# Two chained blocks in float32 on one core: order of work at retention's entry, in attention's last step, and around the norm factors

## The chip, the core and the metric

The program runs on 1 core of a Trainium2 chip. The metric is the device time of one execution in microseconds. The median of three runs is 2414.36 us (2413.3 to 2414.92). The kernel uses five instruction streams: TensorE (PE), VectorE (DVE), ScalarE (ACT), GpSimd (POOL) and SyncE (SP, which only issues transfers). They share SBUF and PSUM and order themselves by semaphores.

## What is computed

The input is x (1024 tokens, width 1024), with two blocks of layers behind each other. Cut to what matters:

```python
def first_block(x, ...):
    p = rms_norm(x, norm_mix_pre) @ w_in
    p_rw, p_ret, g_rw, g_ret = split(p)
    y_rw  = rwkv7_mixer(p_rw, ...)          # 8 heads of 64, chunked recurrence, head norm, gate
    y_ret = retention_mixer(p_ret, pos)     # 8 heads, rotary, decay mask, group norm, silu gate
    merged = sigmoid(g_rw) * (y_rw @ w_branch_rw) + sigmoid(g_ret) * (y_ret @ w_branch_ret)
    h = x + rms_norm(merged @ w_out, norm_mix_post)
    f = (gelu(gate) * val) @ w_down         # gate, val: 3-tap causal convolution of rms_norm(h) @ w_up
    return h + rms_norm(f, norm_ffn_post)

def second_block(x, ...):
    pool_u, pool_gate, q, k, v, attn_gate = split(rmsnorm(x, norm_pre) @ w_in_2)
    pool_out = pool_mixer(pool_u) * silu(pool_gate)
    attn_out = swa_sink_attention(q, k, v, sinks) * silu(attn_gate)   # window 128, 8 heads, 2 kv heads
    y = concat([pool_out, attn_out]) @ w_out_2
    return x + rmsnorm(y, norm_post)
```

## The kernel before

**Layout and products.** Features lie on the 128 partitions, the 1024 tokens along the free axis. Every large product is made from split operands: a float32 number is kept as a high part (`whi`, `xhi`, type fp32r) and a low part (`wlo`, `xlo`), and three matmuls of 128x128 by 512 columns are added in PSUM: high by high, high by low, low by high. A tile of 128 output features over a contraction of 1024 is thus 24 matmuls for each half of 512 tokens.

**Weights.** SP streams blocks of 128x1024 into `wraw` (two slots). POOL splits each: a cast (L402) into `whi` and a subtraction (L404) into `wlo`, then raises `w_ready`. It may overwrite a slot only after PE has raised `w_used` at a matmul of the following block: that is, while PE works from one slot, the other is split. `w_used` is attached to the first matmul of a block, but in the last product of the second block (`last_block`) blocks 0 and 1 are interleaved, and there it comes at the matmul k = 3 of block 0 and k = 4 (`LATE`) of block 1.

**The rwkv stage.** A loop over 4 pairs of heads. In each, PE makes 6 products for the mixer and then 10 later ones (`later_products`) whose matmuls are dealt out one by one as fillings (`fill(n)`) between the small matmuls of the recurrence. Their results go through `psg[0]`/`psg[1]`, are scaled by DVE into `stage` (`normed_half`, L1443) and stored by ACT (`store_later`). At the pair's end come: the sums of squares (L544), DVE's and ACT's head factor, its spread over partitions by 8 transposes (L551), then on DVE the multiply of YB by it (L1558), on ACT scale and bias (L2308), on DVE the addition of the bonus and the gate (L1560, L1562), the store of YB to `yrw_scratch`, and `normed_half` and the store of product 9. YB is a tile of its own name for EN; its last content, of pair 3, stays in SBUF as `yrw[3]`.

**Retention.** `ret_values(p, h)` (L853) brings the values of head h to token order, into `psb`, but for the first pair's head 1 into `psg[1]`, after product 9 has left it. ACT copies them (`values`, L2320), PE turns the keys (`ret_keys`, L860), ACT copies these, PE makes the scores (L886) into `psa` and `psg[1]` and the chunk states (L893), DVE masks the scores (RP, L1609) and runs the states (RS, L1615), PE makes the outputs (L903, L908). Between them stand the matmuls of y_rw @ w_branch_rw as fillings (`fill_branch`, L816). Their operand `xhi` is cast by ACT (L2341), `xlo` subtracted by DVE (`operand_low`, L1595), four each.

**Norm factors.** A factor per token is summed with small matmuls, its root is taken on ACT and DVE, and it is spread to all partitions by transposes (`half_spread`, `spread_of`). These stand between the half blocks of the first products after each norm (`up_block`, `mix_block`, 24 matmuls each, k = 0 to 7).

**Out blocks.** `out_block(n)` is a half tile of merged @ w_out, block 0 waiting before each k for `op_split`, the low half of that feature of `merged` (`merged_low`, L1655).

**Attention.** 16 steps. In each PE makes the scores of the next step, runs 10 fillings, waits for the probabilities (`ap_ready`, DVE L2112), turns them (L1282), runs 6 fillings and multiplies by the values (L1290). The last step, which has no scores to make, runs 24 fillings:

```python
                    else:
                        fill(24 if n == 4 * PAIRS - 1 else 10)
                    pe.wait_ge(sem("ap_ready"), n + 1)
```

The fillings come from one chain of the remaining projections and the first 8 blocks of the last product, in this order: block 0 without k = 7, block 1 with k = 0 to 3, block 0's k = 7, the rest of block 1, blocks 2 to 7.

## Time and profile before

| | us |
|---|---|
| median of 3 runs | 2414.36 |
| lowest, highest | 2413.3, 2414.92 |
| the profiled execution's own time | 2412.11 |
| its span | 2410.3 |
| PE busy | 2356.0 (98%) |
| DVE busy | 1377.7 (57%) |
| POOL busy | 790.9 (33%) |
| ACT busy | 658.0 (27%) |

The profile is of one execution. The times in its rows count from the start of the span; the execution's own time is 1.8 us more than the span. The busy time of PE is counted from modelled ends, so a busy PE may still be one that runs at its lower clock: the windows give the clock that was granted, as a share of 2.4 GHz. In a timeline, a bracket at a row's end gives how long the engine had been idle, and who released it; the same engine's next row shows when it went on.

### The profile page before, as it was taken

What the parts mean: (1) busy time and instruction counts of PE and PEld (TensorE: products, weight loads), DVE (VectorE), ACT (ScalarE), POOL (GpSimd) and SP (SyncE); (2) the same over time, 40 slices, a digit from 0 to 9 for tenths busy, and PEclk for the clock granted to TensorE, in tenths of its full rate; (3) what the DMA queues carried; (4) which work ended last, traced back from release to release, by engine and by line L of the source; (5) the groups of instructions that cost most, each with busy time, mean ns of one, the idle gap of its engine ahead of it and who ended that gap; (6) DMA issues with size and microseconds to landing.
All of it is one profiled execution on the core that took longest, in us unless ns stands there. A gap on an engine that the chain in (4) does not pass through costs nothing.

```text
span 2410.3 us, 33719 instructions
## 1 busy us (share of the span) xinstructions
PE 2356.0 (98%) x12944; PEld 1918.1 (80%) x12944; DVE 1377.7 (57%) x1562; ACT 658.0 (27%) x1064; POOL 790.9 (33%) x420
## 2 busy tenths in 40 slices
PE   7999999999999999999999999999999999999997
PEld 6888888888887887887787788888878787777775
DVE  7755465446545644766558744544541387657766
ACT  4312121121113112443242211111122445114441
POOL 2311231222113114113465333333334445422154
PEclk9999999999999999999999999999999999999998
DMA  3211211121111115645434111111124333211023
GB/s 143 68 53 53 71 55 51 53 71 53 56 59 62 62 45 180 210 145 202 155 130 150 53 47 49 44 52 44 46 76 141 120 120 95 64 63 44 27 79 113
DMA packets 61904, 205.22 MB, mean 85 GB/s; under 512 B 6240, under 2 KB 10464, under 8 KB 61152
## 3 DMA queue, kind: packets, MB, share of 16 engines
q1 hardware_dynamic: 40560, 138.76, 18.5%
q10 hardware_dynamic: 21232, 64.80, 7.3%
q8 instruction: 91, 1.49, 0.3%
q14 instruction: 21, 0.17, 0.0%
HBM read 167.36 MB, written 36.18 MB: 84 GB/s over the span
## 4 chain that ended last, share of the span: by engine, by line
PE 90%; DVE 6%; ACT 2%; DVEq 1%; issue 1%; DMA 0%; POOL 0%; ACTq 0%; POOLq 0%
PE psg L477 10%; PE psg L482 10%; PE psg L481 10%; PE psg L609 7%; PE psg L614 6%; PE psg L616 6%; PE psa L709 1%; PE psg L1205 1%; PE psg L1198 1%; PE psg L571 1%; PE psg L574 1%; PE psg L1203 1%; PE psg L575 1%; PE psb L696 1%; PE psg L1249 1%; PE psg L1243 1%
## 5 line engine op out<-in xcount | busy, mean ns | idle before, releaser
L402 POOL CAST whi<-wraw 128x1024 fp32r<-128x1024 f32 (+1 forms) x176 | 192.2, 1092 | 1397.2 <-PE psg L609 516.8
L404 POOL TENSOR_TENSOR wlo<-wraw,whi 128x1024 fp32r<-128x1024 f32 (+1 forms) x176 | 460.7, 2618 | 25.4 <-issue 0.2
L477 PE MATMUL psg<-xhi,whi 128*128 128x512 f32 x1008 | 401.9, 399 | 3.0 <-issue 1.4
L482 PE MATMUL psg<-xhi,wlo 128*128 128x512 f32 x1008 | 398.3, 395 | 0.0
L481 PE MATMUL psg<-xlo,whi 128*128 128x512 f32 x1008 | 396.0, 393 | 0.0
L609 PE MATMUL psg<-xhi,whi 128*128 128x512 f32 x640 | 261.0, 408 | 0.0
L616 PE MATMUL psg<-xhi,wlo 128*128 128x512 f32 x640 | 259.7, 406 | 0.0
L614 PE MATMUL psg<-xlo,whi 128*128 128x512 f32 x640 | 257.0, 402 | 0.0
L477 PEld LDWEIGHTS psg<-xhi,whi 128*128 128x128 f32 x1008 | 189.2, 188 | 49.1 <-issue 4.5
L482 PEld LDWEIGHTS psg<-xhi,wlo 128*128 128x128 f32 x1008 | 189.2, 188 | 47.7
L481 PEld LDWEIGHTS psg<-xlo,whi 128*128 128x128 f32 x1008 | 189.2, 188 | 46.5 <-issue 0.7
L441 POOL TENSOR_TENSOR wlo<-wraw,whi 128x1024 fp32r<-128x1024 f32 (+1 forms) x50 | 110.9, 2217 | 150.3 <-ACT whi L2480 80.0
L609 PEld LDWEIGHTS psg<-xhi,whi 128*128 128x128 f32 x640 | 120.9, 189 | 26.7 <-issue 6.3
L616 PEld LDWEIGHTS psg<-xhi,wlo 128*128 128x128 f32 x640 | 120.8, 189 | 22.6 <-issue 1.0
L614 PEld LDWEIGHTS psg<-xlo,whi 128*128 128x128 f32 x640 | 121.0, 189 | 19.8
L1786 DVE TENSOR_TENSOR fv<-psg,frs 128x1024 f32<-128x1024 f32 x19 | 23.3, 1225 | 179.5 <-PE psg L482 179.5
L1533 DVE CAST rw_MT<-psa 128x512 fp32r<-128x512 f32 x80 | 55.3, 692 | 83.2 <-PE psa L709 83.2
L1528 DVE TENSOR_TENSOR rw_XM<-psb,mat 128x512 fp32r<-128x512 f32 x80 | 55.3, 692 | 72.6 <-PE psb L696 72.6
L2288 ACT ACTIVATE rw_M<-psb 128x512 fp32r<-128x512 f32 x64 | 38.2, 597 | 204.2 <-PE psb L705 204.2
L2462 ACT ACTIVATE fv<-fv,cp 128x1024 f32<-128x1024 f32 x21 | 26.1, 1244 | 179.2 <-DVE fv L1786 179.2
L1805 DVE TENSOR_TENSOR fparts<-ff,fparts 128x512 fp32r<-128x512 f32 x22 | 17.1, 777 | 93.3 <-ACT fparts L2472 93.3
L1794 DVE SCALAR_TENSOR_TENSOR fg<-fg,cp 128x1022 f32<-128x1022 f32 x20 | 64.0, 3198 | 1.5
(612 smaller groups left out, 4812.8 us busy)
## 6 DMA issues: line engine op xcount, KB each, us to landing
wraw<-w SPq DMA_DIRECT2D x224, 512.0 KB, 3.5
later_scratch<-stage ACTq DMA_DIRECT2D x40, 512.0 KB, 2.6
xres<-xt ACTq DMA_DIRECT2D x4, 1024.0 KB, 10.7
RV<-later_scratch SPq DMA_DIRECT2D x4, 1024.0 KB, 11.4
RG<-later_scratch SPq DMA_DIRECT2D x4, 1024.0 KB, 6.3
later_scratch<-rstage ACTq DMA_DIRECT2D x8, 512.0 KB, 2.6
mgr<-later_scratch ACTq DMA_DIRECT2D x8, 512.0 KB, 3.6
mgt<-later_scratch ACTq DMA_DIRECT2D x8, 512.0 KB, 4.6
```

The source lines that it names most:

```text
L402: pool.tensor_copy(whi[:, u, 0:width], wraw[:, u, 0:width])
L404: pool.tensor_tensor(wlo[:, u, 0:width], wraw[:, u, 0:width], whi[:, u, 0:width].bitcast(F32), ALU.subtract).then_inc(w_ready, 1)
L441: pool.tensor_tensor(wlo[:, u, 0:width], wraw[:, u, 0:width], whi[:, u, 0:width].bitcast(F32), ALU.subtract).then_inc(w_ready, 1)
L477: mm = pe.matmul(ps[:, cols], whi[:, slot, w_cols], rhs_hi(k, cols), start=(k == 0), stop=False)
L481: pe.matmul(ps[:, cols], whi[:, slot, w_cols], rhs_lo(k, cols), start=False, stop=False)
L482: mm = pe.matmul(ps[:, cols], wlo[:, slot, w_cols], rhs_hi(k, cols), start=False, stop=(k == kts - 1))
L609: mm = pe.matmul(ps[:, cols], whi[:, slot, w_cols], xhi[:, k, cols], start=(k == 0), stop=False)
L614: pe.matmul(ps[:, cols], whi[:, slot, w_cols], xlo[:, k, cols], start=False, stop=False)
L616: mm = pe.matmul(ps[:, cols], wlo[:, slot, w_cols], xhi[:, k, cols], start=False, stop=(k == KT - 1))
L1528: tt(XM[:, :, :], bank[2].rearrange("p (q c) -> p q c", q=4), many(M_LVL + lv, 4), MUL).then_inc(sem("x_out"), 1)
L1533: v.tensor_copy(MT[:, :, :], bank[0].rearrange("p (q c) -> p q c", q=4)).then_inc(sem("mt_dve"), 1)
L1794: stt(buf[:, 0, 2:T], taken[:, 0:T - 2], cp[:, 4 * u:4 * u + 1], buf[:, 0, 2:T], MUL, ADD).then_inc(sem("cv_taps"), 1)
```

## The change

It has four parts.

1. Retention's entry. `normed_half(LATER - 1, ...)` is moved ahead of the three multiplies of YB, and its store ahead of ACT's scale and bias. The store of YB moves from the end of a pair to the head of the next one, so that the last pair's YB is not stored at all; slot 0 of `yrw_scratch` takes a tile of zeros, for which a memset is added, and pairs 0 to 2 are read from slots 1 to 3. The four high parts of the branch operand are made by POOL, and two of the low parts too; the other two stay with DVE. POOL makes them before it splits the first branch weights. The `w_used` of the first branch block is attached to the first matmul of `ret_values(0, 0)`.
2. Out blocks 0 and 1 are interleaved as blocks 0 and 1 of the last product are, with `w_used` of block 1 at its k = 4.
3. In the two half blocks `AGAIN + 2` the second spread is moved from behind the block to before its last two k; in `mix_block(0)` the sums are moved from before the last k to before the last two.
4. Attention's last step has 38 fillings instead of 24.

The semaphore counts are adapted (`HIGH_BEFORE`, `SPLIT_BEFORE`). The diff, cut to its core:

```diff
@@ sync
-                sp.dma_start(yrw[r][:, :], yrw_d[:, r, :]).then_inc(sem("yrw_in"), 16)
+                sp.dma_start(yrw[r][:, :], yrw_d[:, r + 1, :]).then_inc(sem("yrw_in"), 16)
             stream(B_BRW, B_BRW + 2, 0)
             sp.wait_ge(g_full, T_BRW)
             load_gates(0)
-            sp.wait_ge(sem("yrw_done"), PAIRS)
+            sp.wait_ge(sem("yrw_done"), PAIRS + 1)
@@ gpsimd, before the branch weights
+            pool.wait_ge(g_full, T_BRW)
+            pool.wait_ge(sem("yrw_in"), 16 * (PAIRS - 1))
+            for j in range(PAIRS):
+                if j == PAIRS - 1:
+                    pool.wait_ge(sem("yrw_done"), PAIRS + 1)
+                pool.tensor_copy(xhi[:, j, :], yrw[j][:, :])
+            pool.drain()
+            for j in range(PAIRS // 2):
+                pool.tensor_tensor(xlo[:, j, :], yrw[j][:, :], xhi[:, j, :].bitcast(F32), ALU.subtract
+                                   ).then_inc(sem("y_pool"), 1)
             split_blocks(B_BRW, B_MRG, PAIRS * P)
@@ tensor, branch_products
-                        pe.wait_ge(sem("op_split"), SPLIT_BEFORE["yrw"] + PAIRS)
+                        pe.wait_ge(sem("y_pool"), PAIRS // 2)
+                        pe.wait_ge(sem("op_split"), PAIRS // 2)
...
-                            if half == 0 and k == 0:
+                            if j and half == 0 and k == 0:
                                 mm.then_inc(w_used, 1)
@@ tensor, ret_values
+                    if p == 0 and h == 0 and c == 0:
+                        mm.then_inc(w_used, 1)
@@ tensor, out blocks
-            for k in range(KT):
+            for k in range(KT - 1):
                 pe.wait_ge(sem("op_split"), SPLIT_BEFORE["merged"] + k + 1)
                 out_block(0, (k,))
-            for n in range(1, KT + 1):
+            out_ready(1)
+            out_block(1, range(LATE), begins=KT)
+            pe.wait_ge(sem("op_split"), SPLIT_BEFORE["merged"] + KT)
+            out_block(0, (KT - 1,))
+            out_block(1, range(LATE, KT), begins=LATE)
+            for n in range(2, KT + 1):
@@ tensor, after the first norm of the feed-forward part (the second block's, with mix_block, likewise)
-            up_block(AGAIN + 2, range(KT // 2, KT)).then_inc(g_full, 1)
+            up_block(AGAIN + 2, range(KT // 2, KT - 2))
             pe.wait_ge(sem("pre_added"), 2 * KT + 1)
             half_spread(1, prstd[:, HALF:T])
+            up_block(AGAIN + 2, range(KT - 2, KT)).then_inc(g_full, 1)
@@ tensor, down1
-            mix_block(0, range(KT - 1))
+            mix_block(0, range(KT - 2))
             pe.wait_ge(sem("down_added"), 2 * KT + 2)
             sums_of(psa[:, 0, :], dacc[:, HALF:T], NB // 2)
-            mix_block(0, range(KT - 1, KT))
+            mix_block(0, range(KT - 2, KT))
@@ tensor, attention
-                        fill(24 if n == 4 * PAIRS - 1 else 10)
+                        fill(38 if n == 4 * PAIRS - 1 else 10)
@@ vector
             v.memset(SC[:, :, :], 0.0)
+            v.memset(YB[:, :], 0.0).then_inc(sem("yrw_done"), 1)
...
                 head_factor(2 * i + 2)
+                for half in range(2):
+                    normed_half(LATER - 1, half)
                 tt(YB[:, :], YB[:, :], flat(psa), MUL).then_inc(sem("gn_nrm"), 1)
                 v.wait_ge(sem("gn_aff"), i + 1)
                 tt(YB[:, :], YB[:, :], BON[:, :], ADD)
                 v.drain()
                 tt(YB[:, :], YB[:, :], G[:, :], MUL).then_inc(sem("yrw_done"), 1)
-                for half in range(2):
-                    normed_half(LATER - 1, half)
...
                 if p == 0:
-                    for j in range(PAIRS):
-                        operand_low("yrw", j, yrw[j][:, :], j)
+                    v.wait_ge(sem("y_pool"), PAIRS // 2)
+                    for j in range(PAIRS // 2, PAIRS):
+                        tt(xlo[:, j, :], yrw[j][:, :], xhi[:, j, :].bitcast(F32), SUB).then_inc(sem("op_split"), 1)
@@ scalar
+                s.wait_ge(sem("yrw_done"), i + 1)
+                s.dma_start(yrw_d[:, bass.ds(i, 1), :].rearrange("p a t -> p (a t)"), YB[:, :]
+                            ).then_inc(sem("yrw_stored"), 16)
...
+                store_later(LATER - 1)
                 s.wait_ge(sem("gn_nrm"), i + 1)
                 act(YB[:, :], YB[:, :], IDN, scale=pp[:, 8:9], bias=pp[:, 9:10]).then_inc(sem("gn_aff"), 1)
-                s.wait_ge(sem("yrw_done"), i + 1)
-                s.dma_start(yrw_d[:, bass.ds(i, 1), :].rearrange("p a t -> p (a t)"), YB[:, :]
-                            ).then_inc(sem("yrw_stored"), 16)
-                store_later(LATER - 1)
...
-            s.wait_ge(sem("yrw_in"), 16 * (PAIRS - 1))
-            for j in range(PAIRS):
-                operand_high(yrw[j][:, :], j)
```

## Rows read from the trace of the kernel before

**Rows 1.** The page's busy table: busy us (share of the span) xinstructions, of TensorE
```profile
PE 2356.0 (98%) x12944; PEld 1918.1 (80%) x12944; DVE 1377.7 (57%) x1562; ACT 658.0 (27%) x1064; POOL 790.9 (33%) x420
```

**Rows 2.** Who TensorE waited for, whole span: us in total, times, longest
```profile
PE psg L571 <- DVE mlo L1655: 1.1, 1, 1.1
```

**Rows 3.** Timeline of PE at retention's entry: start us, duration, [idle before <-releaser]
```profile
954.14 1.95 PE L853 MATMUL psb<-RC,RV 128*128 128x128 f32 x16
...
960.64 3.64 PE L853 MATMUL psg<-RC,RV 128*128 128x128 f32 x16 [4.56 <-DVE stage L1443]
...
965.49 0.34 PE L886 MATMUL psa<-rraw_first 64*128 64x128 f32 x1 [0.33 <-ACT RVT L2320]
...
972.94 2.02 PE L903 MATMUL psb<-RP,RVT 128*128 128x128 f32 x16 [1.51 <-DVE RS L1615]
...
977.48 0.47 PE L816 MATMUL psg<-xhi,whi 128*128 128x512 f32 x1 [0.76 <-DVE xlo L1595]
```

**Rows 4.** Timeline of DVE in the same stretch
```profile
954.34 1.22 DVE L1558 TENSOR_TENSOR rw_EN<-rw_EN,psa 128x1024 f32<-128x1024 f32 x1 [4.12 <-PE psa L551]
...
958.17 1.23 DVE L1562 TENSOR_TENSOR rw_EN<-rw_EN,rw_G 128x1024 f32<-128x1024 f32 x1
...
959.31 1.28 DVE L1443 TENSOR_TENSOR stage<-psg,factor 128x512 f32<-128x512 f32 x2
```

**Rows 5.** Timeline of ACT in the same stretch
```profile
955.59 1.24 ACT L2308 ACTIVATE rw_EN<-rw_EN,pp 128x1024 f32<-128x1024 f32 x1 [6.42 <-DVE rw_EN L1558]
...
961.28 1.02 ACT L2320 ACTIVATE RVT<-psb 128x1024 f32<-128x1024 f32 x1 [4.45 <-DVE stage L1443]
```

**Rows 6.** Timeline of POOL in the same stretch
```profile
917.67 1.04 POOL L402 CAST whi<-wraw 128x1024 fp32r<-128x1024 f32 x1 [19.96 <-PE psg L609]
...
918.85 2.39 POOL L404 TENSOR_TENSOR wlo<-wraw,whi 128x1024 fp32r<-128x1024 f32 x1
...
980.15 3.15 POOL L404 TENSOR_TENSOR wlo<-wraw,whi 128x512 fp32r<-128x512 f32 x1
```

**Rows 7.** Windows: length, busy time of PE, PEld, DVE, ACT, POOL, clock, DMA, GB/s
```profile
960.60:964.10 3.50, 3.46 (x16) 3.46 (x17) 0.06 (x1) 1.02 (x1) 0.00 (x0) 0.51 0.68 273
...
2309.30:2311.00 1.70, 1.68 (x9) 1.69 (x9) 0.00 (x0) 0.00 (x0) 0.00 (x0) 0.50 0.67 267
```

**Rows 8.** Timelines of PE (first two rows) and POOL at out blocks 0 to 2
```profile
1189.56 0.40 PE L571 MATMUL psg<-mhi,whi 128*128 128x512 f32 x1
...
1195.16 0.40 PE L571 MATMUL psg<-mhi,whi 128*128 128x512 f32 x1
...
1184.36 3.26 POOL L404 TENSOR_TENSOR wlo<-wraw,whi 128x1024 fp32r<-128x1024 f32 x1
...
1191.31 2.39 POOL L404 TENSOR_TENSOR wlo<-wraw,whi 128x1024 fp32r<-128x1024 f32 x1
```

**Rows 9.** Timelines of PE and POOL (last row) around attention's last step
```profile
2285.70 1.03 PE L1282 MATMUL psb<-mat,ap__182 128*128 128x128 f32 x8
...
2306.11 0.39 PE L1249 MATMUL psg<-xhi,wlo 128*128 128x512 f32 x1
...
2309.32 1.97 PE L1282 MATMUL psb<-mat,ap__182 128*128 128x128 f32 x8 [2.82 <-DVE ap__182 L2112]
...
2305.32 2.37 POOL L404 TENSOR_TENSOR wlo<-wraw,whi 128x1024 fp32r<-128x1024 f32 x1
```

**Rows 10.** Timelines of PE and DVE (last row) at the second spread
```profile
1319.29 0.60 PE L564 MATMUL psa<-mat,prstd 128*128 128x128 f32 x4
...
1320.77 0.47 PE L571 MATMUL psa<-xhi,whi 128*128 128x512 f32 x1 [0.88 <-DVE frs L1761]
...
1316.76 0.69 DVE L1759 COPY frs<-psa 128x512 f32<-128x512 f32 x1 [1.35 <-PE psa L564]
```

**Rows 11.** Timeline of PE at the sums and spread of down1
```profile
2030.41 1.00 PE L1083 MATMUL psa<-id,dacc 128*128 128x64 f32 x8
...
2032.62 0.66 PE L1090 MATMUL psa<-mat,hexp 128*128 128x128 f32 x4 [0.45 <-DVE hexp L1864]
```

More of the change, by code:

```diff
@@ L50 @@
 QT = T // 4
-SPLIT_BEFORE = {"yrw": 0, "yret": 4, "merged": 12, "cat": 20}
+HIGH_BEFORE = {"yret": 0, "merged": 8, "cat": 16}
+SPLIT_BEFORE = {"yret": 2, "merged": 10, "cat": 18}
 M_ID, M_CENT, M_BLK, M_STRICT, M_INCL, M_LOW0T, M_LVL = 0, 1, 2, 3, 4, 5, 6
@@ L452, in _ @@
             split_blocks(B_P2, B_O2)
-            pool.wait_ge(sem("op_high"), SPLIT_BEFORE["cat"] + LOWS_BY_POOL)
+            pool.wait_ge(sem("op_high"), HIGH_BEFORE["cat"] + LOWS_BY_POOL)
             for j in range(LOWS_BY_POOL):
@@ L1151, in _ @@
             spread_of(psa[:, 1, :], hexp[:, 0:HALF])
-            mix_block(AGAIN + 2, range(KT // 2, KT)).then_inc(g_full, 1)
+            mix_block(AGAIN + 2, range(KT // 2, KT - 2))
             pe.wait_ge(sem("h2_added"), 3)
             spread_of(psa[:, 1, :], hexp[:, HALF:T])
+            mix_block(AGAIN + 2, range(KT - 2, KT)).then_inc(g_full, 1)
             pe.wait_ge(w_ready, B_P2 + AGAIN + 3 + 3)
@@ L1354, in split_low @@
                 for j in range(n):
-                    v.wait_ge(sem("op_high"), SPLIT_BEFORE[name] + j + 1)
+                    v.wait_ge(sem("op_high"), HIGH_BEFORE[name] + j + 1)
                     tt(lo[:, j, :], src[:, j, :], hi[:, j, :].bitcast(F32), SUB).then_inc(sem("op_split"), 1)
@@ L1593, in operand_low @@
             def operand_low(name, n, src, j):
-                v.wait_ge(sem("op_high"), SPLIT_BEFORE[name] + n + 1)
+                v.wait_ge(sem("op_high"), HIGH_BEFORE[name] + n + 1)
                 tt(xlo[:, j, :], src, xhi[:, j, :].bitcast(F32), SUB).then_inc(sem("op_split"), 1)
@@ L1646, in _ @@
                 if p == 0:
-                    v.wait_ge(sem("yrw_stored"), 16 * PAIRS + 16)
+                    v.wait_ge(sem("y_pool"), PAIRS // 2)
                 if p + 1 < PAIRS:
@@ L1652, in merged_low @@
             def merged_low(j):
-                v.wait_ge(sem("op_high"), SPLIT_BEFORE["merged"] + j + 1)
+                v.wait_ge(sem("op_high"), HIGH_BEFORE["merged"] + j + 1)
                 tt(mlo[:, :, j, :], merged[:, :, j, :], mhi[:, :, j, :].bitcast(F32), SUB
@@ L2058, in cat_low @@
                 cols = half_cols(h)
-                v.wait_ge(sem("op_high"), SPLIT_BEFORE["cat"] + h * KT + j + 1)
+                v.wait_ge(sem("op_high"), HIGH_BEFORE["cat"] + h * KT + j + 1)
                 tt(xlo[:, j, cols], cat[:, j, cols], xhi[:, j, cols].bitcast(F32), SUB).then_inc(sem("op_split"), 1)
@@ L2235, in _ @@
                 s.sem_inc(sem(f"stored{b}"), 16)
-            s.sem_inc(sem("yrw_stored"), 16)
             s.wait_ge(sem("rot_stored"), 64)
@@ L2705, in _ @@
                 if j in BY_POOL:
-                    s.wait_ge(sem("y_pool"), BY_POOL.index(j) + 1)
+                    s.wait_ge(sem("y_pool"), PAIRS // 2 + BY_POOL.index(j) + 1)
                 else:
```

## The prediction

> **What bounds the kernel now.** Read the page's busy table first: TensorE (PE) is busy 98% of the span [rows 1], so only what makes PE wait, or makes it slow, can be won. Next the list of who waited for whom on PE: it names few waits, and six of them stand where the change works; one row of that list is shown [rows 2], 1.1 us for the last low half of `merged`. The others stand, with their idle time in brackets, in rows of the timelines, which are read next, PE's first and then those of DVE, ACT and POOL: 4.56 us at retention's entry [rows 3], 2.82 us in attention's last step [rows 9], 0.88 us for `frs` and the same for `drstd` [rows 10], 0.45 us for `hexp` [rows 11]. Everything between these places is matmuls back to back: the 24 of out block 1 take 1195.16 - 1189.56 = 5.60 us [rows 8], 0.233 us each, and that is the unit below ("a matmul"). The first after a wait or a group of small ones costs 0.1 us more.
>
> **Retention's entry.** PE writes the values of head 0 at 954.14, and then stands idle until 960.64, because head 1's go to `psg[1]`, which the last normed half (L1443) frees only after the three multiplies of YB: DVE's order is L1558 954.34, L1560, L1562 958.17, L1443 959.31 to 960.59 [rows 3, 4]. The 16 small matmuls after it take 3.64 us instead of 1.95. The windows say why: the granted clock is 0.51 (the 1.2 GHz level) from 960.6 to 964.1, after an idle stretch of 4.56 us [rows 3, 7].
>
> The change puts L1443 ahead of the multiplies: `psg[1]` is free at 954.34 + 1.28 = 955.6, before PE is through with head 0 (956.1). Head 1 then runs at full clock and ends at about 957.9. What is late next is ACT: YB's first multiply moves to 955.5 to 956.8, ACT's scale and bias (L2308, 1.24 us) to 956.8 to 958.1, and only then the copy of head 0's values (L2320, 1.02 us) ends at 959.2; the copy of head 1 ends at 960.2 [rows 5]. Ahead of them stands only the store that was moved forward. PE turns the keys from 959.3 and begins the scores at 960.35; before, they began at 965.49 [rows 3]. That is 5.1 us. The chain behind it (scores, RP, RS, then head 0 at 972.94 with its 1.51 us wait) has the same links as before, so it moves rigidly: 972.94 becomes 967.8. New idle stretches of 1.4 and 1.6 us remain; after the present one of 1.51 us the next 16 matmuls took 2.02 us, as at full clock, so I count no loss of clock.
>
> The branch products begin at 977.48 now, after 0.76 us for the last xlo [rows 3]. Their high halves move from ACT to POOL, two low halves too. POOL: three casts (1.04 us each) from 953.5, where the last product ends (some 0.6 us before 954.14, the 8 transposes lying between), so under PE's values; the fourth waits for YB, done at 958.17 + 1.23 + 1.28 = 960.7, and ends at 961.8; two subtractions of 2.39 us end at 966.8 [rows 4, 6]; then the first weight block (4 tiles, half as wide, 2.0 us) at 968.9. DVE's two low halves start when RS ends (967.7), 1.2 us each, so 970.2. PE's need is 977.48 - 0.76 - 5.1 = 971.6. Nothing of this is late by these numbers: gain 5.1 + 0.76 = 5.9.
> But DVE and POOL disturb each other on operations between SBUF tiles: POOL's half-wide subtraction at 980.15 took 3.15 us beside DVE's large multiplies [rows 6], against 1.2 us, half of the full-width 2.39 us. DVE's two low halves meet POOL's weight split; if each waits for the other's instruction once, they end at 971.8 to 972.5 and PE waits 0.2 to 0.9 us. I take 5.3 (bounds 3.4, where a disturbance of 3.15 - 1.2 us falls on POOL's own chain as well, to 5.9).
> The Trainium skill bears on this place ("SBUF — State Buffer", section "Who interferes with whom"): a DVE instruction with two SBUF inputs and a GpSimd instruction that reads SBUF cannot share a port pair, and the second to come is blocked until the first ends. By it, RP and RS (one input in PSUM) leave POOL's subtractions alone, and the two low halves cost one blocked turn each: 5.3 rather than 5.9. The row at 980.15 agrees with it.
>
> Of what moves along: the store of YB goes to the head of the next pair (its copy is next written some 25 us after it), and the added memset on DVE falls before the inputs land; I cost both at nothing, 0.5 us at most. Where pair 1's loads waited for `rv_tr` on SP's queue they now wait for YB at 960.7, 3.6 us earlier than now.
>
> **Out blocks 0 and 1.** The wait of 1.08 us before k = 7 goes: block 1's k = 0 to 3 are put there, its weights being ready at 1184.36 + 3.26 = 1187.6. But the signal that releases the weights of block 2 moves from block 1's first matmul to its k = 4. POOL needs from that signal to the end of its subtraction 1191.31 + 2.39 - 1189.56 = 4.14 us [rows 8], and PE has only 12 matmuls, 2.8 us, left. By the steps: block 1 from 1187.7, k = 7 of block 0 from 1190.6, k = 4 of block 1 at 1191.3, weights at 1195.45. Block 2 starts at 1195.5 instead of 1195.16. This part costs 0.3 us (bounds: a loss of 0.8 if DVE blocks POOL once, a gain of 0.8 if the wait turns out hidden).
>
> **Attention's last step.** The last of 24 fillings begins at 2306.11, the next could at 2306.34; PE waits for the probabilities until 2309.32, idle 2.82 us, and comes back at the low clock: the 8 transposes take 1.97 us against 1.03 in an earlier step (0.9 more), and the slow matmuls behind them lose some 0.5 more, so 1.4 us [rows 7, 9]. The 24 are exactly what is left of blocks 0 and 1, so the 14 new ones are all of block 2, whose weights have the same late signal: POOL ends at 2305.32 + 2.37 = 2307.7 [rows 9]. PE idles 1.4 us there, then runs 14 matmuls (3.3 + 0.1 us) to 2311.1. The probabilities are long there; transposes, 6 fillings and the products of the step end at 2314.45 with 20 matmuls of block 2 done, where now they end at 2314.14 with 6. Gain 14 x 0.233 - 0.3 = 2.95 us. Bounds: 1.5 if the clock falls in the shorter gap too, 4.4 if block 2 need not wait. Behind it, cat's low halves come 0.3 us later, and block 8, which needs them, is over 20 us away.
>
> **Spreads inside blocks.** After the second spread (1319.29) PE waits for DVE's copy and starts the last half block at 1320.77: 1.48 us, of which 0.35 is the spread [rows 10]. With 6 matmuls (1.4 us) moved behind the spread the copy is hidden; the moved spread waits for the first copy, done at 1316.76 + 0.69 = 1317.45, and PE reaches it at 1319.29 - 1.4 = 1317.9. Gain 1.0 us here and 1.0 at the twin for `drstd`. DVE starts 1.4 us earlier too, and in the first feed-forward block one wait of PE for it (0.4 us) may go: I add 0.2. At `down1` the sums move from 2030.41 to 2029.7 and 6 matmuls lie between them and the spread, so it starts at 2032.0 instead of 2032.62 [rows 11]: 0.6 us.
>
> **Sum.** 5.3 - 0.3 + 2.95 + 1.2 + 1.0 + 0.6 = 10.75 us. Against the profiled execution (2412.11 us, span 2410.3) that is 2401.4; the runs shown have their median 2.25 us above it, so the median after should be 2414.36 - 10.75 = 2403.6 us.
>
> **Rivals.** (a) The entry gives less: the clock falls in the new gaps of 1.4 to 1.6 us, or POOL and DVE block each other several times. For: the clock is a matter of what PE did before, and PE is only some two thirds busy there. Against: the 2.02 us after the present 1.51 us gap. Half the clock over the 16 + 8 + 32 small matmuls costs some 3 us, and 1.4 us in attention: gain 6.3, 2408.
> (b) The entry gives nothing, because another operand of the branch products (POOL's chain of casts, subtractions and weight split) ends no earlier than 977. It would have to be 5 us slower than its rows; then the rest gives 5.4 less what the clock takes: about 4.5, 2409.9.
> (c) Slower: the late weight signal does not cost one wait but is handed on. If POOL's split took longer than a block, each of the 14 further out blocks would start 1.35 us late, 19 us against 10.75 gained: 2422. It decides from the point where a split (4.14 us from the signal) exceeds a block's 5.60 us. Against: later blocks give their signal with the first matmul, and 1.46 us of slack swallow the delay within one block.
> (d) More: block 2 of attention does not wait and nothing is blocked: 5.9 + 4.4 + 0 + 2.8 = 13.1, 2401.3.
>
> **How the numbers follow.** Forecast 0.70, (a) 0.15, (b) 0.07, (c) 0.02, (d) 0.06. A difference under about 0.2% (4.8 us) can't be told from no change. Faster: the forecast, (a), (d) = 0.91; within: (b) = 0.07; slower 0.02. The range takes the forecast's own width (8.5 to 12.5 us) and half of (a): 2401.0 to 2408.0.
>
> **What would show it.** Right: scores start some 5.1 us nearer to head 0's values than now, those of head 1 take 1.95 us; a new wait of PE of about 1.4 us on POOL's wlo at out block 2, and another in attention; none for `frs`, `drstd`, `hexp`; no stretch at the low clock in either place. Wrong: a wait for xlo or wlo of over 1 us before the first branch product, a clock below 1 behind a gap of 1.5 us, or waits on wlo at out blocks 3 and later.

## The result

| kernel | executions timed | median us | lowest to highest | profiled execution us | its span |
|---|---|---|---|---|---|
| before | 5 | 2414.36 | 2413.3 to 2415.09 | 2412.11 | 2410.3 |
| after | 5 | 2400.73 | 2400.37 to 2401.49 | 2401.04 | 2399.2 |

The kernel after is faster: the ratio of the medians is 0.9944, with a 95% interval of 0.9929 to 0.9958. The gain is 13.6 us where 10.75 were forecast, and 2400.73 lies 0.27 us below the low end of the range. Between the two profiled executions the gain is 2410.3 - 2399.2 = 11.1 us.

Busy time of the engines in the profile after, which answers to [rows 1]. PE's busy time is 4.2 us less though it issues the same 12944 instructions: most of that goes with the 6.8 us at the low clock that are no longer there (half of them is 3.4 us).

```profile
PE 2351.8 (98%) x12944; PEld 1914.9 (80%) x12944; DVE 1373.2 (57%) x1561; ACT 654.3 (27%) x1060; POOL 800.0 (33%) x426
```

Who TensorE waited for in the kernel after (us in total, times, longest), the rows of the places that the change touches. The rows for `stage`, `mlo` [rows 2], `frs`, `drstd`, `hexp` and the branch's `xlo` are gone; the waits for weights have grown, for `wlo` at L582 (out blocks) from 0.2 to 1.4 us and at L1264 (attention) from 0.7 to 1.9 us.

```profile
PE psb L917 <- DVE RS L1637: 3.0, 4, 1.5
...
PE psb L874 <- ACT RVT L2342: 2.0, 4, 1.3
PE psg L1264 <- POOL wlo L405: 1.9, 2, 1.2
...
PE psg L582 <- POOL wlo L405: 1.4, 2, 1.2
...
PE psg L488 <- DVE fg L1809: 0.4, 1, 0.4
```

PE's timeline at retention's entry, after. Against [rows 3]: head 1's values follow head 0's at once and take 1.99 us, the keys are turned from 959.91, the scores begin at 960.93, and the first branch product comes at 972.18 without a wait of its own.

```profile
954.88 1.95 PE L865 MATMUL psb<-RC,RV 128*128 128x128 f32 x16
956.66 1.99 PE L865 MATMUL psg<-RC,RV 128*128 128x128 f32 x16
959.91 1.09 PE L874 MATMUL psb<-mat,RKD 128*128 128x128 f32 x8 [1.26 <-ACT RVT L2342]
960.93 0.37 PE L900 MATMUL psa<-rraw_first 64*128 64x128 f32 x1
...
968.41 2.02 PE L917 MATMUL psb<-RP,RVT 128*128 128x128 f32 x16 [1.54 <-DVE RS L1637]
...
972.18 0.48 PE L828 MATMUL psg<-xhi,whi 128*128 128x512 f32 x1
```

DVE's timeline there, after. The stage goes first and YB's three multiplies behind it; lower, the two low halves of the branch operands take 2.31 and 1.62 us, though 1.2 us is what such a tile took in the kernel before, without POOL beside it: they lie beside POOL's weight split. They end at 972.03, just before PE wants them.

```profile
955.25 1.29 DVE L1465 TENSOR_TENSOR stage<-psg,factor 128x512 f32<-128x512 f32 x2 [4.29 <-PE psa L562]
956.46 1.21 DVE L1582 TENSOR_TENSOR rw_EN<-rw_EN,psa 128x1024 f32<-128x1024 f32 x1
...
968.18 2.31 DVE L1642 TENSOR_TENSOR xlo<-yrw,xhi 128x1024 fp32r<-128x1024 f32 x1
970.41 1.62 DVE L1642 TENSOR_TENSOR xlo<-rw_EN,xhi 128x1024 fp32r<-128x1024 f32 x1
```

POOL's timeline there, after: the fourth cast waits for YB, and two subtractions end at 967.44. The last row is a piece of the weight split that began 0.04 us before DVE's first low half.

```profile
961.57 1.04 POOL L440 CAST xhi<-rw_EN 128x1024 fp32r<-128x1024 f32 x1 [4.33 <-DVE rw_EN L1586]
962.75 4.69 POOL L443 TENSOR_TENSOR xlo<-yrw,xhi 128x1024 fp32r<-128x1024 f32 x2
...
968.14 1.26 POOL L405 TENSOR_TENSOR wlo<-wraw,whi 128x512 fp32r<-128x512 f32 x1
```

Windows of the kernel after (length, busy us of PE, granted clock, DMA share, GB/s): the clock stays at 1.00 through the entry and through attention's last step, where [rows 7] have 0.51 and 0.50. The idle stretches that are left there (1.26, 1.54 and 1.25 us) were followed by no fall.

```profile
955.00:961.00 6.00, 4.74 (x43) 1.00 0.75 262
961.00:965.00 4.00, 4.00 (x65) 1.00 0.63 193
...
2300.00:2304.00 4.00, 4.00 (x23) 1.00 0.48 131
```

PE's timelines of the kernel after at out block 2, at attention's block 2 and transposes [rows 8, 9], and at the second spread [rows 10], which comes at full clock with matmuls right behind it.

```profile
1189.76 0.50 PE L582 MATMUL psg<-mhi,whi 128*128 128x512 f32 x1 [1.22 <-POOL wlo L405]
...
2299.46 0.50 PE L1264 MATMUL psg<-xhi,whi 128*128 128x512 f32 x1 [1.25 <-POOL wlo L405]
...
2302.83 1.04 PE L1303 MATMUL psb<-mat,ap__182 128*128 128x128 f32 x8
...
1312.61 0.60 PE L575 MATMUL psa<-mat,prstd 128*128 128x128 f32 x4
1314.44 0.40 PE L582 MATMUL psa<-xhi,whi 128*128 128x512 f32 x1
```

Step by step, by setting each matmul of one PE timeline beside the same one of the other and reading how the distance in time changes:

| place | forecast us | measured us |
|---|---|---|
| start, loop heads, up to the entry | 0 | -0.7 |
| retention's entry | +5.3 | +6.0 |
| pairs 1 to 3 of retention | 0 | +0.4 |
| out blocks | -0.3 | -0.4 |
| spreads `pre`, `h2` | +1.0, +1.0 | +1.1, +1.1 |
| first feed-forward block's wait | +0.2 | 0 |
| `down1` | +0.6 | +0.75 |
| attention | +2.95 | +2.9 |
| sum | 10.75 | 11.1 |

So the profiled executions leave 0.4 us to explain, and the medians 2.9. What has to be found out is mainly why the runs of before lie 2.25 us above its profiled execution, and those of after 0.3 below.

### The profile page after: what moved, and what is told of

It reads as the page before. It is cut to its first block, busy times and chain, and to the rows that moved or that the text cites. A ratio compares the mean times of both kernels' runs of the same rounds, so it can differ in the third digit from the quotient of the medians.

```text
span 2399.2 us, 33722 instructions
## 1 busy us (share of the span) xinstructions
PE 2351.8 (98%) x12944; PEld 1914.9 (80%) x12944; DVE 1373.2 (57%) x1561; ACT 654.3 (27%) x1060; POOL 800.0 (33%) x426
## 4 chain that ended last, share of the span: by engine, by line
PE 89%; DVE 6%; ACT 2%; DVEq 1%; issue 1%; DMA 0%; POOL 0%; ACTq 0%; POOLq 0%
PE psg L493 9%; PE psg L488 9%; PE psg L492 9%; PE psg L620 7%; PE psg L625 6%; PE psg L627 6%; PE psa L720 1%; PE psg L582 1%; PE psg L1226 1%; PE psg L1219 1%; PE psg L585 1%; PE psg L586 1%; PE psg L1224 1%; PE psb L707 1%; PE psg L1268 1%; PE psg L1270 1%
## 5 line engine op out<-in xcount | busy, mean ns | idle before, releaser
L1828 DVE TENSOR_TENSOR fparts<-ff,fparts 128x512 fp32r<-128x512 f32 x22 | 17.1, 778 | 93.3 <-ACT fparts L2491 93.3
## 6 DMA issues: line engine op xcount, KB each, us to landing
xres<-xt ACTq DMA_DIRECT2D x4, 1024.0 KB, 11.1
RV<-later_scratch SPq DMA_DIRECT2D x4, 1024.0 KB, 11.1
```

## Experiments

Two theories. **Clock theory:** the two long idle stretches of before, 4.56 and 2.82 us, make TensorE's clock fall in some executions more than in others, so a typical execution is slower than the profiled one; after has no such stretch. **Session theory:** the 2.25 us belong to the few runs shown, or to something common to them, and have nothing to do with the change. The kernels of the table were timed in three sessions, each beside the kernel before (e0 is that kernel as well, timed as one of the others): 29 executions of it with a median of 2413.53 us (2410.77 to 2416.09), then 9 with 2412.57 (2411.12 to 2413.33), then 20 with 2413.0 (2411.17 to 2414.97).

| kernel | executions | median us | lowest to highest | profiled | gain on before, same session |
|---|---|---|---|---|---|
| e0 before again | 11 | 2412.84 | 2410.75 to 2415.12 | 2410.80 | 0.7 |
| e1 entry alone | 7 | 2406.34 | 2404.45 to 2408.36 | 2405.22 | 7.2 |
| e2 fillings alone | 11 | 2410.07 | 2408.4 to 2411.04 | 2409.73 | 3.5 |
| e4 spreads alone | 11 | 2410.14 | 2407.64 to 2411.54 | 2410.51 | 3.4 |
| e9 after | 5 | 2400.42 | 2399.49 to 2402.32 | 2402.32 | 12.2 |
| e5 after, old out blocks | 5 | 2399.98 | 2399.04 to 2400.66 | 2400.66 | 12.6 |
| e6 after, k = 0, 1 first | 5 | 2399.98 | 2398.91 to 2400.95 | 2400.95 | 12.6 |
| e7 e6 and 3 in attention | 5 | 2399.37 | 2397.57 to 2399.93 | 2399.37 | 13.2 |
| e3 out blocks alone | 11 | 2412.93 | 2409.16 to 2415.06 | 2412.97 | 0.1 |
| e8 after, 24 fillings | 6 | 2404.91 | 2402.17 to 2406.36 | 2402.17 | 8.1 |
| e10 after, old order | 9 | 2406.34 | 2405.36 to 2408.58 | 2407.64 | 6.7 |
| e11 entry and fillings | 5 | 2403.51 | 2402.65 to 2405.05 | 2402.65 | 9.5 |

**e0, the kernel before again.** No edit.

> The kernel before, unchanged, to see the scatter of its executions and a second profile of it. In the first profile it has an execution of 2412.11 us, 2.25 us below the median of its runs, while the kernel after has 2401.04 us in its profile and 2400.73 us as median. Clock theory: the idle stretches of 4.56 us (retention's entry) and 2.82 us (attention's last step) let TensorE's clock fall for a time that differs from run to run, and the first profile holds a short case. Then this profile shows either stretches at the low clock of another length or place, or a time near 2412, and the runs scatter over 2412 to 2415.5, more than those of after (1.1 us). Session theory: the difference of 2.25 us belongs to something common to a chip or a session (DMA, start), so the profile and the runs here agree within 0.7 us, at any level, and the low-clock stretches are those of the first profile.

The scatter is as wide as the clock theory has it, 4.4 us over 11 executions, and the profile, 2410.80 us, is 1.3 us below the first one. Its PE timeline differs from the first by one step of that size, in attention. PE idles as long as before, but comes back at full clock (transposes 1.09 us, not 1.97 [rows 9]); the window has the clock at 1.00. At the entry it is the low clock again.

```profile
2309.40 1.09 PE L1282 MATMUL psb<-mat,ap__182 128*128 128x128 f32 x8 [2.91 <-DVE ap__182 L2112]
```

Two windows of e0 (length, busy time of PE, PEld, DVE, ACT, POOL, clock, DMA share, GB/s):

```profile
2308.00:2311.00 3.00, 1.60 (x11) 1.50 (x12) 1.27 (x2) 0.47 (x1) 0.10 (x1) 1.00 0.54 175
960.00:964.00 4.00, 3.82 (x21) 3.82 (x22) 0.20 (x2) 1.28 (x2) 0.00 (x0) 0.59 0.64 254
```

**e1, e2 and e4, one part each in the kernel before.** e1 has the edits of the entry, e2 the one line in attention, e4 the moved sums and spreads:

```diff
# e2
-                        fill(24 if n == 4 * PAIRS - 1 else 10)
+                        fill(38 if n == 4 * PAIRS - 1 else 10)
# e4, one of three places
-            up_block(AGAIN + 2, range(KT // 2, KT)).then_inc(g_full, 1)
+            up_block(AGAIN + 2, range(KT // 2, KT - 2))
             pe.wait_ge(sem("pre_added"), 2 * KT + 1)
             half_spread(1, prstd[:, HALF:T])
+            up_block(AGAIN + 2, range(KT - 2, KT)).then_inc(g_full, 1)
```

> The kernel before with retention's entry alone from the change. The step by step comparison of the two profiles gives the entry 6.0 us and 0.4 us more in the pairs behind it. Clock theory: the median falls by 6.4 us and by about 1 us more, since the idle stretch of 4.56 us with its low clock goes: 7.0 to 8.0 us, near 2407. Session theory: 6.0 to 6.7 us, near 2408. Both: head 1's 16 value products take 1.95 us and not 3.64, and there is one stretch at the low clock left, in attention's last step.

> The kernel before with the 38 fillings alone from the change. The profiles give them 2.9 us. Clock theory: the median falls by 2.9 us and by up to 1.2 us more, 3.3 to 4.2 us, near 2410.5; session theory: 2.7 to 3.1 us, near 2411.5. Both: a wait of 1.2 us for the weights of block 2 in place of one of 2.8 us, transposes in 1.04 us and not in 1.97, and one stretch at the low clock left, at retention's entry.

> The kernel before with the spreads and sums inside blocks alone from the change (pre, down1, h2). The profiles give 1.11 + 0.75 + 1.11 = 2.97 us. Both theories on the clock say the same here, 2.7 to 3.2 us and a median near 2411.4, since no stretch at the low clock is touched: if the median falls by clearly more or less, neither is right, and the offset between profile and runs comes from elsewhere. The wait of 0.4 us in the first feed-forward block stays.

The medians fall by 7.2, 3.5 and 3.4 us. e1 and e2 lie where the clock theory wants them, but e4 is 0.2 us above its own bound too, and e0, which changes nothing, gains 0.7 in the same session: the medians can't decide between the theories, which differ by about as much. The profiles say more: each part makes the steps of the table above (entry 5.9, spreads 1.1 and 1.1, `down1` 0.6), so the parts add up. Against e0, which had no fall in attention either, e1's profile is 2410.80 - 2405.22 = 5.6 us faster. In e4 the clock fell for twice as long at the entry, 6.8 us and not 3.4: the keys are turned at the low clock as well, and by the end of the scores that has cost 0.9 us more than in the first profile. In PE's timeline of e4:

```profile
960.39 3.79 PE L853 MATMUL psg<-RC,RV 128*128 128x128 f32 x16 [4.56 <-DVE stage L1445]
963.97 1.92 PE L860 MATMUL psb<-mat,RKD 128*128 128x128 f32 x8
```

In e0's, with the same idle stretch:

```profile
960.18 3.53 PE L853 MATMUL psg<-RC,RV 128*128 128x128 f32 x16 [4.56 <-DVE stage L1443]
963.55 1.04 PE L860 MATMUL psb<-mat,RKD 128*128 128x128 f32 x8
```

In e1, which keeps attention's idle stretch (2.92 us), the clock did not fall there. Both theories had expected a low stretch there.

**e9, the kernel after again.** No edit.

> The kernel after, unchanged, as the base for the three beside it, and to see its scatter on this chip. Clock theory: it has no idle stretch of over 1.6 us left between the first matmuls and the last layer, so its runs lie within 1.5 us of each other (2400.2 to 2401.7, median 2400.8), with no stretch at the low clock between start and tail, while the kernel before, run beside it, scatters over some 4 to 5 us. Rival: the narrow scatter of the five runs seen was chance; then the runs here spread over 3 us or more as well.

The expectation of a narrow scatter fails: five executions over 2.8 us, beside 2.2 us for nine of before. No fall of the clock shows between start and tail in the profile; it is the slowest of the five, and 0.9 of its 1.3 us over the first profile come before retention's entry, in the first 80 us and at the heads of the mixing loop, where each kernel's profiles differ by a few tenths to 1.2 us. So the start scatters in every kernel, and the narrow runs of the result (1.1 us over five) were chance, as the rival has it. With those of the result, after has ten executions with a median of 2400.66.

**e5, e6 and e7, the out blocks, in the kernel after.** e5 puts back the old order; e6 moves the late signal forward, e7 also that of attention:

```diff
# e6
+OUT_LATE = 2
...
-            out_block(1, range(LATE), begins=KT)
+            out_block(1, range(OUT_LATE), begins=KT)
...
-            out_block(1, range(LATE, KT), begins=LATE)
+            out_block(1, range(OUT_LATE, KT), begins=OUT_LATE)
# e7, beside it (attention's interleave)
-LATE = 4
+LATE = 3
```

> The kernel after with out blocks 0 and 1 in the order of before (all of block 0, then block 1). By the profiles the change lost 0.39 us here (a wait of 1.08 us went, two for the weights of 1.22 and 0.2 us came): this kernel is 0.4 us faster than after, near 2400.4. Rival: the wait for the weights has a cause of its own and stays, then it is 0.7 to 1.1 us slower.

> The kernel after with only k = 0 and 1 of out block 1 ahead of k = 7 of block 0 (after: k = 0 to 3), so that the signal which releases the weights of block 2 comes 1.4 us earlier. In the profile of after POOL starts on them 0.3 us after that signal and needs 3.55 us, and PE waits 1.22 us; with the signal at 1184.4 they are ready at 1188.1 and PE comes at 1188.4. mlo's last tile is ready at 1183.0 and wanted at 1183.4. So no wait at either place: 1.2 us faster than after, near 2399.5, and 0.8 us faster than the kernel without the interleave. Rival: DVE's last low half (2.23 us instead of 1.22) ends later or POOL is disturbed; then a wait of 0.3 to 1 us comes at one of the two places and the gain is 0.2 to 0.9.

> As the one before, and also in the last step of attention with three instead of four k of block 1 ahead of k = 7 of block 0. The signal for block 2's weights comes 0.7 us earlier, but cat's low half for k = 7 is ready at 2294.2 and now wanted at 2293.85: a wait of 0.35 us, and the wait of 1.25 us for the weights shrinks by as much as the signal gains, 0.35. Net 0 to 0.4 us faster than the one before, near 2399.3. Rival: it costs as much as it gives, since the same 24 matmuls stand between; then equal within 0.2 us.

By the medians all three are faster than e9, by 0.4, 0.4 and 1.05 us, each within the scatter; the steps in the profiles are sharp. e5: the wait for mlo is back (1.09 us), those for the weights are gone, net 0.41 us faster, as expected. e6: out block 2 comes 1.36 us nearer, more than the 1.2 expected. POOL starts on its weights earlier and is through in time:

```profile
1185.75 1.04 POOL L404 CAST whi<-wraw 128x1024 fp32r<-128x1024 f32 x1 [2.84 <-PE psg L583]
1186.94 2.40 POOL L406 TENSOR_TENSOR wlo<-wraw,whi 128x1024 fp32r<-128x1024 f32 x1
```

e7 adds 0.2 us, the lower half of the 0 to 0.4 expected: in attention the wait for `wlo` shrinks from 1.25 to 0.54 us, and one of 0.24 us for cat's low half comes. Two rows of its PE timeline:

```profile
2292.86 0.50 PE L1265 MATMUL psg<-xhi,whi 128*128 128x512 f32 x1 [0.24 <-DVE xlo L2084]
...
2297.86 0.50 PE L1265 MATMUL psg<-xhi,whi 128*128 128x512 f32 x1 [0.54 <-POOL wlo L406]
```

e7 has the lowest median and the lowest execution of all kernels here (2399.37, 2397.57), and by the steps it is 1.6 us faster than after; five executions each can't set it apart from after by their times alone.

**e3, the out blocks alone, in the kernel before.** The edit is the change's own in that place.

> The kernel before with the interleave of out blocks 0 and 1 alone from the change. By the steps between the two profiles it loses 0.39 us (a wait of 1.08 us for mlo goes, two for the weights, 1.22 and 0.2 us, come). That is a tenth of the scatter of the runs of before, so the medians can't show it; the profile can: out block 1's 24 matmuls and those of block 2 later by 0.3 to 0.5 us than in a profile of before, counted from block 0. Rival: on its own it gains up to 0.8 us.

As expected from the profile: +1.08 us for mlo, -1.48 for the weights, net -0.4; the medians (2412.93 and 2413.0) show nothing.

```profile
1195.61 0.50 PE L571 MATMUL psg<-mhi,whi 128*128 128x512 f32 x1 [1.21 <-POOL wlo L404]
```

**e8 and e10, one idle stretch put back, in the kernel after.**

```diff
# e8
-                        fill(38 if n == 4 * PAIRS - 1 else 10)
+                        fill(24 if n == 4 * PAIRS - 1 else 10)
# e10, DVE (on ACT the store of the last half goes back behind gn_aff as well)
-                for half in range(2):
-                    normed_half(LATER - 1, half)
                 tt(YB[:, :], YB[:, :], flat(psa), MUL).then_inc(sem("gn_nrm"), 1)
...
                 tt(YB[:, :], YB[:, :], G[:, :], MUL).then_inc(sem("yrw_done"), 1)
+                for half in range(2):
+                    normed_half(LATER - 1, half)
```

> The kernel after with 24 fillings instead of 38 in attention's last step, so the idle stretch of 2.9 us is back, alone. Clock theory: after it the clock falls in some executions and not in others (it fell in two of the four profiles that had this stretch, and each fall cost 1.3 us), so the runs spread over at least 2 us and form two heaps 1.3 us apart: about 2402.0 without a fall and 2403.4 with one; the median is 1.6 to 3.0 us above that of after. Rival: the spread of runs has nothing to do with this stretch; then the runs lie within 1.5 us, 2.9 us above after.

> The kernel after with the last normed half and its store back behind the multiplies of YB, so that the idle stretch of 4.6 us at retention's entry is back, alone; POOL still makes the high halves and two low halves of the branch operands. The scores start 4.8 us later, as before, and the 0.76 us wait for xlo stays away: 4.6 to 5.4 us slower than after, near 2405.5. Clock theory: a fall of the clock follows in every profile with this stretch (four of four), three times of 3.4 us and once of 6.8 us, so the runs spread by some 1.5 to 3 us. Rival: within 1.5 us.

e8 scatters widely, over 4.2 us, and its median lies 8.1 us under before where after's lies 12.2 under: by these medians, of six and five executions in different sessions, the stretch costs 4.1 us, more than the 1.6 to 3.0 expected. Two heaps 1.3 us apart don't show. Its profile, the fastest of the six, has no fall and ends 1.2 us behind the first profile of after (2400.4 against 2399.2): it is 0.4 us ahead up to attention and loses 1.6 there. So without a fall the 14 more fillings are worth 1.6 us, and not 2.9. e10 costs 12.2 - 6.7 = 5.5 us by the medians, 0.1 over the expectation, with 3.2 us of scatter; its profile has a fall of 6.8 us, and loses 6.1 us to after's at the entry. A window of e10 (busy us of PE, clock, DMA share, GB/s):

```profile
961.00:967.00 6.00, 5.40 (x24) 0.50 0.30 110
```

**e11, entry and fillings in the kernel before.** The edits of e1 and e2 together.

> The kernel before with retention's entry and the 38 fillings, without the interleaved out blocks and without the moved spreads. Both long idle stretches are gone. Clock theory: its runs lie as close together as those of after (within 2 us; the kernel before spreads over 5 us), and its median is after's 2400.6 less the 0.4 us of the out blocks plus 2.97 us of the spreads: 2403.2. The gain against before is then 10 us by the medians, though the profiles give the two parts only 6.4 + 2.9 = 9.3. Rival: the scatter is that of before.

Median 2403.51 against 2403.2 expected, 9.5 us under before; the scatter of 2.4 us is wider than 2, and is that of e9. The two parts together give what they give in the profiles, 9.3 us. No extra beyond that is shown by this kernel.

**Four single executions, profiled**, to see a slow execution from inside: l1 and l2 are the kernel before, l3 and l4 are e8.

> The kernel before, unchanged, one more profile. Its runs reach from 2410.8 to 2416.1 us; profiles so far: 2410.8 with one stretch of 3.4 us at the low clock (entry), 2412.1 with two. Clock theory: time = about 2409.1 us plus half of the low-clock time behind the two idle stretches, give or take 0.7 us from the start: one stretch of 3.4 us gives 2410.8, 3.4 + 3.4 gives 2412.5, 6.8 + 3.4 gives 2414.2. Rival: a time above 2413.5 with no more than two stretches of 3.4 us, and the loss found elsewhere.

> As the one before: the kernel before, unchanged, one more profile, with the same two expectations.

> The kernel after with 24 fillings instead of 38 in attention's last step, one more profile. Its six runs reach from 2402.2 to 2406.4 us, and the one profile, 2402.17, has no fall of the clock. Clock theory: 2402.2 plus half of the low-clock time behind the idle stretch of 2.9 us, give or take 0.7 us: none 2402.2, 3.4 us 2403.9, 6.8 us 2405.6. Rival: a time above 2404 without a fall of the clock, or with one of 3.4 us only.

> As the one before: the kernel after with 24 fillings, one more profile, with the same two expectations.

l1 took 2412.80 us, l2 2413.36, l3 2404.14, l4 2404.10. l3 and l4 show attention's part. Both have the fall that e8's own profile hasn't, after the same idle stretch, and stand 2.0 us behind it: 1.45 to 1.6 for the slow matmuls and some 0.45 a few blocks later, where a wait for weights of 0.18 us now shows. Their times, 2404.14 and 2404.10, lie within the clock theory's 2403.9 give or take 0.7, but also just within the rival's "above 2404". PE of e8, the execution without a fall:

```profile
2300.75 1.09 PE L1303 MATMUL psb<-mat,ap__182 128*128 128x128 f32 x8 [2.91 <-DVE ap__182 L2135]
2301.60 0.48 PE L1264 MATMUL psg<-xhi,whi 128*128 128x512 f32 x1
```

PE of l3, the same program with the fall (a matmul takes 0.43 us from start to start, not 0.23):

```profile
2300.77 1.17 PE L1303 MATMUL psb<-mat,ap__182 128*128 128x128 f32 x8 [2.82 <-DVE ap__182 L2135]
2301.62 0.75 PE L1264 MATMUL psg<-xhi,whi 128*128 128x512 f32 x1
2302.17 0.63 PE L1268 MATMUL psg<-xlo,whi 128*128 128x512 f32 x1
```

The windows 2301 to 2304 of e8 and, in the second fence, of l3:

```profile
2301.00:2304.00 3.00, 3.00 (x30) 2.45 (x28) 0.00 (x0) 2.12 (x4) 1.61 (x2) 1.00 0.34 138
```

```profile
2301.00:2304.00 3.00, 3.00 (x14) 2.40 (x12) 0.00 (x0) 2.03 (x4) 1.32 (x2) 0.61 0.35 137
```

l1 and l2 add what the clock theory had left out. Both have the same two falls as the first profile, for which it gave 2412.5 give or take 0.7 (l2 lies outside), and yet are 0.7 and 1.25 us slower: 0.7 and 0.9 of it come in one place behind attention, where in l2 POOL's cast takes 2.93 us instead of the 1.50 of the first profile, and PE then waits 0.57 us for the weights (0.43 in l1, not at all in the first profile and in e0). POOL of the first profile, POOL of l2, and PE's wait in l2:

```profile
2319.01 1.50 POOL L402 CAST whi<-wraw 128x1024 fp32r<-128x1024 f32 x1 [3.56 <-PE psg L1243]
```

```profile
2319.28 2.93 POOL L402 CAST whi<-wraw 128x1024 fp32r<-128x1024 f32 x1 [3.67 <-PE psg L1243]
```

```profile
2325.05 0.50 PE L1243 MATMUL psg<-xhi,whi 128*128 128x512 f32 x1 [0.57 <-POOL wlo L404]
```

DVE has eight subtractions beside this cast. Where the cast took 1.50 us they took 7.95, and where it took 2.93 they took 4.89 (4.89 in l1 too): in one execution DVE was held up, in the others POOL. DVE of the first profile, then of l2:

```profile
2315.92 7.95 DVE L2060 TENSOR_TENSOR xlo<-cat,xhi 128x512 fp32r<-128x512 f32 x8
```

```profile
2316.09 4.89 DVE L2060 TENSOR_TENSOR xlo<-cat,xhi 128x512 fp32r<-128x512 f32 x8
```

## Why the prediction was right and where it was wrong

**Right: the places, the mechanisms and nearly every size.** PE no longer waits for the stage, and ACT's copy of the values is what is late next (1.26 us), then RS (1.54), both at full clock. The out blocks trade one wait for another and lose 0.4 us, for the reason given, the signal at k = 4; e6 shows that by moving it. Attention gains 2.9 us with a new wait of 1.25 us for block 2's weights. The spreads give 1.1 each. By the medians before and after differ by 13.6 us with an interval of 10.1 to 17.1 (from the ratio's), in which 10.75 lies.

**Small misses in the sum, 0.4 us.** The entry gave 6.0 and not 5.3. The disturbance of DVE's two low halves that I took off did happen (2.31 and 1.62 us where 1.2 each were free), but they ended at 972.03 while PE came at 972.18: hidden, so the unblocked value of 5.9 held. (The Trainium skill, "SBUF — State Buffer", section "Who interferes with whom", has whoever issues second wait for the other's whole instruction; the 2.31 us agree with that, since POOL's subtraction of 968.14 ends at 969.40, and DVE's ends 1.1 us later.) Pairs 1 to 3 of retention gave 0.4 us that the sum hasn't: PE's wait for RS in pair 1 fell from 0.89 to 0.49 us, and why was not followed up. The start and the loop heads took 0.7 us, and differ as much between two profiles of one kernel. The wait for DVE in the first feed-forward block stayed at 0.4 us.

**Wrong: the last line of the sum.** It reads "the runs shown have their median 2.25 us above it, so the median after should be 2414.36 - 10.75 = 2403.6 us". This step put the distance between a median and one profiled execution in as if it belonged to the kernel and stayed with it through a change. The runs show that it doesn't. The 2.25 us come apart as follows.
- About 1.2 us: the runs shown stood high. With the three sessions the kernel before has 74 timed executions with a median of 2413.1. All five of the result lie above that; whether by chance or by something common to them is not shown.
- About 1.0 us: the profiled execution stood low. l1 and l2, with the same falls of the clock, are 0.7 and 1.25 us slower, through the wait for weights behind attention and, in l2, the start.
- For the kernel after the distance is -0.4 us (2400.66 over ten executions against 2401.04). Neither part carried over.

Had the sum been left on the execution it was worked out for, 2412.11 - 10.75 = 2401.36 us, it would have been 0.6 off, in part by luck: over all executions the medians differ by 2413.1 - 2400.66 = 12.4 us, 1.3 more than the two profiles (11.1). That rest is no larger than the distance between two profiled executions of one kernel (2410.80 to 2413.36 for before, 2401.04 and 2402.32 for after), and nothing here says what it is made of. The range took in the sizes of the steps (8.5 to 12.5 us, so down to 2401.9) and its low end left 0.9 us more, less than this distance, although the distance was a fifth of the gain and the three runs shown already spread over 1.6 us.

**The clock.** My clock theory is right that the fall varies from execution to execution, and is not shown to be what the 2.25 us are made of. Shown: after an idle stretch of 2.8 to 2.9 us the clock falls in some executions of one program and not in others, at a price of 1.3 us (e0 against the first profile) to 2.0 us (l3, l4 against e8); after 4.56 us it fell in each of the eight profiles that had it, in e4 and e10 for 6.8 us instead of 3.4. So removing such a stretch gains more or less by the execution. The prediction's 2.95 us for attention counted the fall as certain (1.4 of them); that fits the execution that it was worked out for, but in e0, e1 and e8, 3 of the 10 profiles with that stretch, there was no fall, and by e8 1.6 us are then left to gain. Not shown: that the falls explain the 2.25 us. e11 gains no more than its profile steps, and e9 scatters as before does in its session.

**Open.** Two of e8's six executions took 2406.35 us, 4.2 us above its fastest; the profiles account for 2.0 of it, and no profile was had of such an execution. A fall of twice the length would cost about as much again, but that is only argued. That e4's median gained 3.4 us where its steps give 2.9 is left to scatter.

## What to carry to other kernels

Work out a change against the profiled execution, don't add that execution's distance from the median as if it were exact, and widen the range by how far executions of one program lie apart (here 1 to 5 us in 2413); more than one profile of the kernel before shows what in the sum comes and goes, as the clock's fall in attention did here. When one block's tail is put inside the next, look first at which signal moves with it: putting only as many matmuls ahead as the late operand needs (two k instead of four) turned a loss of 0.4 us into a gain of 1.0. And where two engines hold each other up, the price counts only as far as it passes the consumer's own arrival.

## What the hardware showed that was not expected

- An idle stretch of TensorE of 2.82 to 2.92 us went either way: the clock fell around its end in the profiles of before, e3, e4, l1, l2, l3 and l4, and not in those of e0, e1 and e8. At idle stretches of 1.54 us or less it never fell in these profiles, between the first matmuls and the tail. The Trainium skill ("TensorE: Matmul & The Clock Gate", section "What's actually happening") states of a kernel's start that the count of slow matmuls differs between runs of the same kernel; the profiles here show the like of a fall in its middle.
- After the same 4.56 us the low clock lasted 3.4 us in most profiles and 6.8 us in two (e4, e10), so one cause has two prices, 0.9 us apart at this place.
- One and the same cast on POOL took 1.50 us in one execution of before and 2.93 in another, while DVE's eight subtractions beside it took 7.95 and 4.89 us; the second became a wait of PE of 0.57 us. Two executions of one program differ in which engine is held up by the other.
